# First block's output projection, second norm and first expert queries done 128 tokens at a time in plain fp32

## The reference, cut to what matters

```python
o_gla = rms_norm(o_gla, gla_norm_g) * silu(r_g)
o_swa = rms_norm(o_swa, swa_norm_g)
x = x + gate1 * (concatenate([o_gla, o_swa]) @ w_out)   # 1024 x 1024
h2 = modulate(x, norm2_g, shift2, scale2)               # second norm
q = h2 @ w_peer_q                                       # 8 heads, 2 halves of 128
s1, s2 = q_half1 @ keys_1, q_half2 @ keys_2             # 128 keys each
# per token and head: top 16 of each, top 16 of the 16 x 16 sums -> 16 experts of 16384
x = x + gate2 * sum_e gate_e * gelu(h2 . u[e]) * v[e]   # 128 experts for each token
```

## Time and profile before

| | us |
|---|---|
| median of 3 runs | 1480.06 (1479.98 to 1480.14) |
| span of the profiled execution | 1480.7 |
| PE busy | 1311.9 (89%) |
| DVE busy | 933.9 (63%) |
| ACT busy | 655.4 (44%) |
| share of DMA in the chain that ended last | 27% |
| moved by DMA | 422.51 MB |

### The profile page before, as it was taken

One profiled execution on the slowest core, in us unless ns is written; L12 is line 12 of the kernel. 1 busy time (PEld: TensorE's weight loads), 2 busy tenths in 40 slices (PEclk: granted clock), 3 DMA queues, 4 the chain that ended last, 5 costly groups with the idle time before them and its releaser, 6 DMA issues.

```text
span 1480.7 us, 21207 instructions
## 1 busy us (share of the span) xinstructions
PE 1311.9 (89%) x6932; PEld 936.0 (63%) x6932; DVE 933.9 (63%) x2248; ACT 655.4 (44%) x1801; POOL 390.6 (26%) x432
## 2 busy tenths in 40 slices
PE   6999979888988777878777887999999998999998
PEld 3889934444443222333222476999998987899897
DVE  6678586766667667667754555655556635655555
ACT  3434434344343333333333335545455248544554
POOL 4111144444544444444444142200001005100000
PEclk9999999999999999999999998999999999999999
DMA  8875599999999999999999621665556630445554
GB/s 332 333 254 200 182 422 420 421 421 421 421 421 422 421 422 421 422 421 422 421 422 421 268 89 37 234 219 182 182 182 238 196 102 14 157 149 188 187 185 144
DMA packets 81341, 422.51 MB, mean 285 GB/s; under 512 B 10144, under 2 KB 11472, under 8 KB 48368
## 3 DMA queue, kind: packets, MB, share of 16 engines
q0 software_dynamic: 46656, 303.71, 50.1%
q1 hardware_dynamic: 33280, 114.68, 23.3%
q10 hardware_dynamic: 1328, 3.15, 0.6%
HBM read 418.88 MB, written 2.62 MB: 285 GB/s over the span
## 4 chain that ended last, share of the span: by engine, by line
PE 55%; DMA 27%; DVE 8%; ACT 5%; issue 2%; POOL 1%; DVEq 0%; ACTq 0%; SPq 0%; POOLq 0%
DMA big<-in_experts,R 26%; PE pacc L1136 8%; PE pu L663 6%; PE pu L664 6%; PE pu L665 6%; PE pu L632 3%; DVE big L2380 3%; PE pu L644 2%; PE pacc L663 2%; PE pacc L664 2%; PE pacc L665 2%; PE pacc L720 2%; PE pacc L722 2%; PE pacc L721 2%; ACT L1455 1%
## 5 line engine op out<-in xcount | busy, mean ns | idle before, releaser
L1136 PE MATMUL pacc<-big,early_l 128*128 128x512 f32 x1024 | 492.7, 622 | 119.5 <-ACT early_l L1455 119.2
L1136 PEld LDWEIGHTS pacc<-big,early_l 128*128 128x128 f32 x1024 | 188.1, 195 | 408.4 <-issue 406.1
L2380 DVE CUSTOM_DVE_ANT_0 big<-big,early_h 128x1024 f32<-128x1024 f32 x256 | 311.8, 1224 | 204.9 <-DMA big<-in_experts,R 203.8
L535 POOL DMA_INDIRECT big<-in_experts,R x256 | 288.1, 1125 | 378.7 <-PE pacc L1136 334.3
L436 DVE TENSOR_TENSOR ring_lo<-ring,ring_hi 128x512 fp32r<-128x512 f32 x328 | 214.7, 696 | 195.0 <-ACT ring_hi L429 194.9
L429 ACT ACTIVATE ring_hi<-ring 128x512 fp32r<-128x512 f32 x328 | 187.6, 620 | 123.5 <-PE pu L665 49.4
L1455 ACT ACTIVATE R<-R 128x1 f32<-128x1 f32 x256 | 51.6, 202 | 322.3 <-DVE R L2380 322.1
L663 PE MATMUL pu<-X2h,ring_hi 128*128 128x256 f32 x512 | 146.2, 286 | 3.2 <-DVE big L2497 3.2
L665 PE MATMUL pu<-X2h,ring_lo 128*128 128x256 f32 x512 | 145.6, 284 | 0.0
L664 PE MATMUL pu<-X2l,ring_hi 128*128 128x256 f32 x512 | 145.4, 284 | 0.0
L663 PEld LDWEIGHTS pu<-X2h,ring_hi 128*128 128x128 f32 x512 | 98.9, 193 | 4.2 <-DVE big L2497 3.6
(11 more groups left out here) (408 smaller groups left out, 2097.4 us busy)
## 6 DMA issues: line engine op xcount, KB each, us to landing
ring<-in_weights SPq DMA_DIRECT2D x216, 512.0 KB, 3.5
big<-in_ada POOLq DMA_DIRECT2D x40, 512.0 KB, 6.3
big<-in_w POOLq DMA_DIRECT2D x12, 512.0 KB, 7.1
big<-in_experts,R POOLq DMA_INDIRECT x256, 20.0
bias_row<-big ACTq DMA_DIRECT2D x1, 1536.0 KB, 19.8
XT<-in_xT ACTq DMA_DIRECT2D x1, 1024.0 KB, 8.2
scr<-in_ada POOLq DMA_DIRECT2D x2, 512.0 KB, 12.3
tk<-in_ada POOLq DMA_DIRECT2D x2, 512.0 KB, 14.0
```

What stands on the lines that cost most here:

```text
L535: pool.indirect_dma_start(out=pair_rows[:, m % PAIR_SLOTS, :], out_offset=None, in_=experts_d, in_offset=bass.IndirectOffsetOnAxis(ap=expe ...
L1136: last = mm(paccf[:, tt * D + half * 512:tt * D + (half + 1) * 512], diagonal[:, m % 16, :], pair_rows[:, m % PAIR_SLOTS, D + half * 512:D ...
L2380: v.tensor_tensor_reduce(out=pair_rows[:, m % PAIR_SLOTS, 0:D], in0=pair_rows[:, m % PAIR_SLOTS, 0:D], in1=h2_rows[:, u % TT, :], scale=1. ...
```

## The change

- `w_out` leaves the ring. It has its own tensor in HBM and its own place `wout` in SBUF: the buffers of expert pairs 6 to 9. SP loads it in two halves of four 512 KB transfers: the first after the exponentials of the linear attention (`ex_done`), between ring slots 11 and 12; the second after its scores (`gla_scores`), ahead of ring slots 18 to 21, which are now the first four of `peer_q`.
- All eight parts of the output projection run in plain fp32 by tile (`out_tile`), `i` from 0 to 7. All of tile 0 comes first; its norm sums go in between. The splits of `w_out` and `os_` are gone. `os_` is scaled by tile.
- Queries 0 to 3 run by tile. For tile 0 they are done before the pairs. The order of units starts (head 0, tile 0), (head 1, tile 0), (head 0, tile 1), (head 1, tile 1).
- Tile 1's output projection runs on PE after tile 0's queries; DVE adds its results in between the steps of lists 0 and 1. Its norm, queries, scores and transposes run at given places behind pairs 0 to 14 (`second_tile`). POOL issues pairs 0 to 5 and then waits for all 16 parts of the projection.
- Queries 4 to 15 start at pair 20 in place of 0.

```diff
-_COUNTS = [("w_in", 18), ("w_out", 8), ("peer_q", 16), ("a_in", 4), ...
+_COUNTS = [("w_in", 18), ("peer_q", 16), ("a_in", 4), ...
...
+FIRST_QUERY = 20
+UNIT_ORDER = [(0, 0), (1, 0), (0, 1), (1, 1)] + [(h, tt) for h in range(2, PH) for tt in range(TT)]
+EARLY_PAIRS = 6
...
+            rounds(1, 3)
+            sp.wait_ge(s["consts_made"], 1)
+            sp.wait_ge(s["ex_done"], 1)
+            out_weights(0)
+            rounds(3, 4)
+            for n_slot in range(16, 18):
...
+            sp.wait_ge(s["gla_scores"], 1)
+            out_weights(1)
+            for n_slot in range(18, 20):
...
                 if m % TOPK == 0:
                     pool.wait_ge(s["listed"], m // TOPK + 1)
+                if m == EARLY_PAIRS:
+                    pool.wait_ge(s["out_tiles"], 16)
...
+            out_tile(0, 0)
             pe.wait_ge(s["squares"], SQUARED["gla"])
...
+            out_tile(1, 0)
             pe.wait_ge(s["inverses"], 2)
...
+            gla_spread(0)
+            out_tile(2, 0)
+            gla_spread(1)
+            for i in range(3, 6):
                 out_tile(i, 0)
...
+            h2_sums(0, range(0, 2))
+            out_tile(6, 0)
+            h2_sums(0, range(2, 4))
+            out_tile(7, 0)
+            h2_sums(0, range(4, C))
             h2_spread(0)
...
             tile_query(0, 0)
+            tile_query(1, 0, range(0, 4))
             tile_scores(0, 0)
+            tile_query(1, 0, range(4, C))
+            tile_query(2, 0)
             tile_scores(1, 0)
+            h2_turn(0, 0)
+            h2_turn(0, 1)
+            tile_query(3, 0)
+            tile_scores(2, 0)
+            tile_scores(3, 0)
+            for i in range(8):
+                out_tile(i, 1)
...
+            def second_tile(m):
+
+                if m == 0:
+                    h2_sums(1, range(C))
+                elif m == 1:
+                    h2_spread(1)
+                elif m == 3:
+                    tile_query(0, 1)
+                elif m == 4:
+                    tile_query(1, 1)
+                elif m == 5:
+                    tile_scores(0, 1)
+                elif m == 6:
+                    tile_scores(1, 1)
+                elif m in (7, 8):
+                    h2_turn(1, m - 7)
+                elif m == 10:
+                    tile_query(2, 1)
+                elif m == 12:
+                    tile_query(3, 1)
+                elif m == 13:
+                    tile_scores(2, 1)
+                elif m == 14:
+                    tile_scores(3, 1)
...
             gate_exp(0)
...
+            for i in range(4, C):
+                h2_square(i, 1)
...
-                if m == 3:
+                if m == 0:
                     gate_exp(1)
+                    h2_root(1)
+                elif m == 2:
+                    h2_shift(1)
...
             key_lists(0)
             pair_search(0)
             pair_experts(0)
+            tile_residual(0, 1)
+            tile_residual(1, 1)
             unit_gates(0)
-            dve.wait_ge(s["h2_copied"], 2)
+            key_lists(1)
+            tile_residual(2, 1)
+            tile_residual(3, 1)
+            pair_search(1)
+            tile_residual(4, 1)
+            tile_residual(5, 1)
+            pair_experts(1)
+            tile_residual(6, 1)
+            tile_residual(7, 1)
...
+                if m == 1:
+                    h2_inverse(1)
+                elif m == 2:
+                    h2_tile(1)
+                elif m == 3:
+                    unit_gates(1)
```

More of the change, by code:

```diff
@@ L968, in out_tile @@
             def out_tile(i, tt):
[L970 to L975, removed]
+                if tt == 0 and i % 4 == 0:
+                    pe.wait_ge(s["wout_loaded"], 16 * (i + 4))
+                if i == 0:
+                    pe.wait_ge(*((s["out_inputs"], 1) if tt else (s["normed"], NORM["swa"])))
+                elif i == 4:
+                    pe.wait_ge(s["out_inputs"], tt + 2)
@@ L976, in out_tile @@
+                if tt and i >= 4:
+                    pe.wait_ge(s["out_added"], C + i // 2 * 2 - 2)
+                elif tt == 0 and i >= 2:
+                    pe.wait_ge(s["out_added"], i - 1)
+                elif tt == 0:
+                    pe.wait_ge(s["evacs"], USE["w_in"] + 17 + i)
+                x = os_ if i < 4 else og
                 for j in range(2):
                     for c in range(4):
-                        last = mm(pu[:, e % 2, j * T + tt * P:j * T + (tt + 1) * P], slot(n)[:, c * T + j * P:c * T + (j + 1) * P],
-                                  og[:, c, tt * P:(tt + 1) * P], start=(c == 0), stop=(c == 3))
@@ L980, in out_tile @@
[L980 to L994, removed]
@@ new lines, in h2_sums, with h2_spread @@
+            def h2_sums(tt, chunks):
+                for c in chunks:
+                    pe.wait_ge(s["x_sq"], 4 * tt + c // 2 + 1)
+                    last = mm(h2_sum(tt), sq[:, c, tt * P:(tt + 1) * P], ones[:, 0:1],
+                              start=(c == 0), stop=(c == C - 1), skip_group_check=True)
+                if C - 1 in chunks:
+                    last.then_inc(s["sums"], 1)
+            def h2_spread(tt):
+                pe.wait_ge(s["inverses"], 3 + tt)
+                if tt == 0:
+                    pe.wait_ge(s["normed"], NORM["gla"])
+                mm(h2_rows_spread(tt), over_columns(stats[:, 12 + tt:13 + tt]), ident[:, :], start=True, stop=True)\
+                    .then_inc(s["spreads"], 1)
@@ L1048, in query, with tile_query @@
                 last.then_inc(s["slots_used"], 1)
[L1050 to L1054 removed]
+            def tile_query(i, tt, chunks=range(C)):
+                n, e = SLOT["peer_q"] + i, query_use(i, tt)
+                if 0 in chunks:
+                    if tt == 0:
+                        wait_slot(n)
                     pe.wait_ge(s["evacs"], e - 1)
[L1056 to L1058 removed]
+                for c in chunks:
@@ L2126, in _ @@
             last.then_inc(s["states_ready"], 1)
[L2128 to L2129 removed]
+            swa_scaled(1).then_inc(s["out_inputs"], 1)
             dve.wait_ge(s["inter_psum"], 1)
```

420 lines of the change are left out of this document (192 added, 228 removed).

## The result

| | before | changed |
|---|---|---|
| median of 20 runs each, us | 1479.48 (1478.02 to 1481.55) | 1483.03 (1480.46 to 1485.79) |
| span of the profiled execution, us | 1480.7 | 1479.2 |
| first pair issued | 177.36 | 169.19 |
| last pair issued, landed | 815.86, 836.20 | 816.06, 837.35 |

The ratio is 1.0022, with an interval of 1.0015 to 1.0028: the change makes the kernel slower by 3.5 us, 0.2%. That is small, but the interval is clear of 1. I had forecast 1473.7, faster, with a range up to 1478.5. Direction and range are wrong.

A forecast was written before the change was run, and what follows sets the result against it. DMA was taken to bound the stream of 256 expert pairs, with room ahead of it. Terms -12.1 + 3.7 + 1.5 + 0.5 = -6.4 us gave 1473.7 us from 1480.06; range 1469.8 to 1478.5.

The forecast's parts named there:

- The start: Ahead of the pair stream: first pair issued at 165.3 instead of 177.36, -12.1 us, give or take 1.5.
- The early loads: `w_out` and other loads moved ahead of the stream might delay DVE's modulation rows: 0 to +5 us, taken as +0.5.
- Rival 2: Window attention and near 118 us: early loads make a modulation row late and hold up DVE, +7, 1480 us; 8%.
- The head: First pairs of the stream: buffers come free with little margin, so DMA runs partly dry; +1.5 us, between 0 and +6.
- the upper bound: At the head: +6 us, if PE runs pairs 1 to 3 at the lower clock.
- rival 4: At the head: idle PE gets half clock for six pairs, with sums and queries among them doubled; +14, 1488 us; 7%.
- The ring loads: In the pair stream: twelve `peer_q` loads instead of nine, three more at 1.25 us each, +3.7 us.
- Rival 3: Ahead of pair 1: idle drains beside ACT's three table loads delay the twelfth pair by 3.8, 1477.5 us; 4%.

The follow-up runs named there:

- run 2: Changed kernel plus products of zeros that keep PE busy at the head (50 after tile 1's last projection part, 20 after pairs 0 and 2): 1476.92 us, ratio 0.9982.
- run 5: Changed kernel with both zero products at the head and the next query weights loaded only after the second reciprocal: 1475.09 us, ratio 0.9974.
- run 9: run 5 with three of the stream's ring loads (slots 22 to 24) cut to 16 of 1,024 columns: 1473.39 us, ratio 0.9961.
- run 1: The changed kernel once more, no edit: 1484.67 us, ratio 1.0032.
- run 3: Changed kernel with the first four query weights (2.1 MB) held back until behind the second reciprocal: 1481.40 us, ratio 1.0013.
- run 10: run 5 plus 4 zero products ahead of the product that spreads tile 0's inverse and 8 behind it: 1473.84 us, ratio 0.9955.
- run 7: Control: the kernel before, with 20, 10 and 8 zero products behind its first three pairs: 1479.04 us, ratio 0.9997.

## Why the prediction was wrong

This table shows the stream alone: how many us after the first pair the n-th is issued, from POOL's timelines.

| pair | before | changed | run 2 | run 5 | run 9 |
|---|---|---|---|---|---|
| 12 | 17.1 | 30.2 | 25.1 | 25.1 | 25.1 |
| 26 | 54.5 | 70.9 | 67.3 | 65.6 | 65.6 |
| 41 | 94.8 | 107.4 | 103.8 | 102.1 | 102.1 |
| 101 | 249.5 | 257.2 | 252.2 | 252.1 | 251.5 |
| 256 | 638.5 | 646.9 | 642.0 | 641.6 | 640.5 |

**The start (-12.1, measured -8.2 and, in run 1, -4.1).** The mechanism of the gain was right: tile 1's norm is out of the path, `out_tile(0,0)` starts at 127.93 (128.1 expected), DVE waits 1.30 us for the second half of the scores (1.3), and the list after it takes the time I gave it. Two terms were missing. First, I let the spread follow `out_tile(1,0)` at once, at 133.8; it came at 135.52, because the reciprocal stands behind a late modulation row. In the first profile PE would hardly have been earlier by itself, since `out_tile(1,0)` took 3.06 us there and ended only 0.45 ahead; but in run 2 it took 2.03, PE then waited 1.29 us for the reciprocal, and the spread still came at 135.37. The row was late because it waits for four rows behind SP's second half of `w_out` and the query weights, in engines that were full; run 3 takes the query weights away and the row is there 4.4 us earlier. That is near the 5.0 us that their 2.1 MB take at 421 GB/s. "Ahead of the stream DMA has room" was true of the average and not of these 12 us. With what follows, the norm sums of tile 0 ended at 151.3, not 148.8. Second, PE ran the first queries in part at half clock behind two short waits (0.55 and 0.97 us): 4.53 us, where run 10 needs 3.33. The sum is 3.9 us: 169.19 instead of 165.3.

**The early loads (+0.5).** The step failed in its place. The first half of `w_out`, at 69 us, cost nothing that shows at 128; I had set its bound there, and for the second half I wrote that the waits of DVE stand before 118.64 and that two ring loads leave that stretch. I had not followed the late rows, which POOL loads right behind, through the same queues. Rival 2 names this mechanism, transfers of SP's queue that stretch POOL's rows, but put it in the window attention and at 118. The Trainium skill, "DMA: Bandwidth & Descriptors", Queues, rings and completion order, says that a DMA engine takes turns between the queues that have work for it; the 13.39 us of the row, and its return to 129.76 in run 3, agree.

**The head (+1.5, measured 5 and some 2 more).** This is the step that turned the sign: run 2, which takes away the half clock alone, is below the kernel before, and run 3, which takes away the late row alone, is not. The order of events was as written: the seventh pair late without harm, the second added late, the twelfth waiting. At full clock the times were right too. By my sum the second pair is added, and so the twelfth goes out, 25.9 us after the first (191.2 less 165.3); in run 2 it is 25.1, in the changed kernel 30.2 and 28.3. I saw that PE would stand idle and kept the lower clock for the upper bound and for rival 4, and took the low end "since later pairs have PE time to spare". That argument is about how a loss grows, not about whether there is one, and nothing in it kept PE's clock up. The profile of the kernel before already showed the half clock at 192 to 196 behind a shorter idle time; there it was free (run 7), here the additions of the first two pairs were the release for pairs 11 and 12. Rival 4 had the cause and three times the price: it doubled six pairs and all the sums and queries among them, while the clock came back at about 200 us. I gave it 7%.

Even at full clock the head is not free. In run 9, without the three ring loads, the stream is 2.0 us longer than before (640.5 against 638.5). At pair 26 it stands 11 us behind, and 4 of these are regained by pair 41 and 5 more by pair 101, while the kernel before still carries its own ring loads. Which of tile 1's steps sets this pace was not separated. The last pair also takes 21.3 us from issue to landing in all changed kernels, 20.3 before and in run 7; where that comes from is open. These pieces nearly give the growth of the stream of 9.3 us (658.8 to 668.2): 4.9 for the clock, 1.2 for the ring loads, 2.0 for the head at full clock, 1.0 for the last pair's way.

**The ring loads (+3.7, measured 0.6 and 1.2).** The count was right, the price was not. I charged bytes at the full rate of the stream, but the three loads that I took out fall into the stretch where the engines set the pace. So terms of my sum were not independent: where the head waits for the engines, bytes cost next to nothing. The price of a ring load later in the stream was not measured. So the mis-sized term is +3.7, of which 0.6 and 1.2 came.

**The functions of ACT.** Rival 3 did not happen: the loads take 1.28 us each, and the exponential starts at 187.06, 0.02 after its load has ended. The Trainium skill, "ScalarE: Activation LUTs", What ACT_TABLE_LOAD costs, adds a drain; no run here shows it.

Together, in the profiled execution: start +3.9, stream 668.2 us against the 664.0 of my sum, +4.2, early loads -0.5. That is 7.6 us, and the last landing is at 837.35 instead of 829.8. What follows the landing, which the change leaves as it is, happened to take 641.9 us in this execution and 644.5 in the one of before (640.1 to 644.5 over all fourteen profiles, so the one of before is the longest), and its span is 4.9 above my 1474.3 and not 7.6. Its time stands 1.7 above that span, where I had carried over 0.6 below, and the median is 2.2 above its time. In every execution of which both are on record the time is 1.6 to 1.8 us above the span; by that, an estimate, the profiled execution of the kernel before, with a span of 1480.7, was itself 2.8 to 3.0 us longer than the median of 1479.48. So a part of the miss of 9.3 us is the spread of single executions, and I had one to judge the median by.

The range was also added up a little too wide: by its own terms it goes from 1470.2 (1471.7 less 1.5) to 1478.2 (1473.7 and 4.5 more), not from 1469.8 to 1478.5. The result lies outside either.

## What to carry to other kernels

When a change opens idle time on PE ahead of work that others wait for, cost that work at half clock from the start, and ask which buffer it releases. Zero products in the idle time are a cheap remedy (90 of them gave 6 us or more here), but only where the work behind them is waited for; and look at the granted clock of more than one execution (12 of them at the start kept it in one of three). When loads are moved ahead, follow every other transfer of that stretch, by whatever queue, to the statement that stands behind it, and look how many transfers its semaphore counts.

## What was not expected of the hardware

- Queues that are idle on the average can be full for long enough: 8 ring and `w_out` transfers of 512 KB beside four late rows filled the DMA engines from 120 to 132 us (share 1.02) and took the last row from 6.3 us (the median before) to 13.39, and DVE, in order, passed 4.56 us of idle time on to a reciprocal that had nothing to do with it.
- Two executions of the same kernel get different clocks in the same place: PE's 16 products behind the first spread took 3.58 us in run 1 and 1.95 in the first profile, the queries 5.46 and 4.53. The changed kernel's 20 runs spread over 5.3 us, the kernel before's over 3.5.
- Cutting three transfers of 512 KB in a stretch at 418 GB/s moved none of the first 34 pairs by more than 0.1 us (runs 5 and 9): a rate that looks full is not always the bound.
